# Retention's rotated queries and keys: 32x32 squares on VectorE and DMA moves in place of TensorE transposes

## The reference

```python
q = rotary(q.reshape(shp).astype(F32))                       # 256 tokens, 4 heads of 128
k = rotary(k.reshape(shp).astype(F32)) * (RET_HD ** -0.5)
...
scores = jnp.einsum("bhqd,bhkd->bhqk", qi, ki) * mask[None]
out = (jnp.einsum("bhqk,bhke->bhqe", scores, vi)
       + jnp.einsum("bhcd,bhde->bhce", qi * q_dec_f, state))
...
o = (o - mu) * lax.rsqrt(jnp.mean(jnp.square(o - mu), axis=-1, keepdims=True) + EPS)
```

## Time and profile before

| | us |
|---|---|
| median of 3 runs | 1694.01 (1693.87 to 1696.77) |
| span of the profiled execution | 1692.8 |
| TensorE busy | 1670.1 (99%) |
| VectorE busy | 1152.0 (68%) |
| ScalarE busy | 968.3 (57%) |
| span less TensorE busy | 22.7 |

### The profile page before, as it was taken

One profiled execution on the slowest core, in us unless ns is written; L12 is line 12 of the kernel. 1 busy time (PEld: TensorE's weight loads), 2 busy tenths in 40 slices (PEclk: granted clock), 3 DMA queues, 4 the chain that ended last, 5 costly groups with the idle time before them and its releaser, 6 DMA issues.

```text
span 1692.8 us, 24538 instructions
## 1 busy us (share of the span) xinstructions
PE 1670.1 (99%) x10066; PEld 1383.8 (82%) x10066; DVE 1152.0 (68%) x1835; ACT 968.3 (57%) x1522; POOL 19.9 (1%) x54
## 2 busy tenths in 40 slices
PE   9999999999999999999999999999999999999998
PEld 7778888887888888888888888888888888888886
DVE  6887875778788667555676578655575556985554
ACT  7845554577374447444667676544464456975443
POOL 1000000010000000000000000000000000000000
PEclk9999999999999999999999999999999999999999
DMA  7323355542244555455544335555555555455553
GB/s 265 125 82 132 147 183 187 178 169 107 77 168 162 180 196 188 178 195 177 210 185 153 134 124 177 218 194 190 208 192 194 181 217 187 149 187 180 193 180 143
DMA packets 41872, 291.67 MB, mean 172 GB/s; under 512 B 4673, under 2 KB 4929, under 8 KB 7713
## 3 DMA queue, kind: packets, MB, share of 16 engines
q1 hardware_dynamic: 39312, 280.68, 46.0%
q0 software_dynamic: 2304, 8.91, 1.5%
q10 hardware_dynamic: 144, 0.52, 0.1%
HBM read 289.05 MB, written 1.05 MB: 171 GB/s over the span
## 4 chain that ended last, share of the span: by engine, by line
PE 84%; DVE 10%; ACT 3%; issue 1%; DMA 1%; SPq 0%; DVEq 0%; ACTq 0%
PE pg L535 21%; PE pg L538 21%; PE pg L536 21%; PE pg L485 4%; PE pg L487 3%; PE pg L486 3%; DVE wl L2004 3%; PE ps L843 2%; PE ps L678 2%; DMA raw<-weights 1%; ACT wh L1339 1%; PE ps L892 1%; PE ps L662 1%; PE ps L964 0%; DVE hTl L2603 0%
## 5 line engine op out<-in xcount | busy, mean ns | idle before, releaser
L2004 DVE TENSOR_TENSOR wl<-raw,wh 128x1024 fp32r<-128x1024 f32 x494 | 581.3, 1220 | 183.7 <-ACT wh L1339 180.6
L535 PE MATMUL pg<-wh,hTh 128*128 128x512 f32 x1676 | 661.0, 394 | 1.3 <-ACT arena L1391 1.0
L538 PE MATMUL pg<-wh,hTl 128*128 128x512 f32 x1676 | 653.4, 390 | 0.0
L536 PE MATMUL pg<-wl,hTh 128*128 128x512 f32 x1676 | 652.5, 389 | 0.0
L1339 ACT ACTIVATE wh<-raw 128x1024 fp32r<-128x1024 f32 x522 | 522.8, 1054 | 201.7 <-DMA raw<-weights 191.4
L538 PEld LDWEIGHTS pg<-wh,hTl 128*128 128x128 f32 x1676 | 314.5, 188 | 67.0 <-DVE hTl L2070 0.3
L535 PEld LDWEIGHTS pg<-wh,hTh 128*128 128x128 f32 x1676 | 314.8, 188 | 64.0 <-ACT arena L1391 1.4
L536 PEld LDWEIGHTS pg<-wl,hTh 128*128 128x128 f32 x1676 | 315.0, 188 | 62.2
L485 PE MATMUL pg<-wh,hTh 128*128 128x512 f32 x416 | 171.4, 412 | 2.2 <-DVE wl L2004 2.2
L1445 ACT ACTIVATE arena<-pg,sm 128x256 f32<-128x256 f32 (+1 forms) x67 | 36.6, 547 | 237.4 <-PE pg L538 237.3
L487 PE MATMUL pg<-wh,hTl 128*128 128x512 f32 x416 | 163.0, 392 | 0.0
(11 more groups left out here) (406 smaller groups left out, 1322.7 us busy)
## 6 DMA issues: line engine op xcount, KB each, us to landing
raw<-weights SPq DMA_DIRECT2D x265, 1024.0 KB, 4.8
arena<-wide POOLq DMA_DIRECT2D x9, 512.0 KB, 3.7
raw<-weights SPq DMA_DIRECT2D x2, 512.0 KB, 6.4
cst<-const_tables POOLq DMA_DIRECT2D x1, 1024.0 KB, 5.3
plainh<-dist_tables POOLq DMA_DIRECT2D x2, 512.0 KB, 6.2
arena<-gate_mix POOLq DMA_DIRECT2D x1, 1024.0 KB, 8.3
x<-x_in ACTq DMA_DIRECT2D x1, 512.0 KB, 3.9
x<-x_in SPq DMA_DIRECT2D x1, 512.0 KB, 9.5
```

The lines of the kernel that those rows point to most:

```text
L535: pe.matmul(dst, high, wh[:, slot, at], start=start, stop=False)
L536: pe.matmul(dst, high, wl[:, slot, at], start=False, stop=False)
L538: return pe.matmul(dst, low, wh[:, slot, at], start=False, stop=stop)
L2004: tt(wl[:, slot, h], raw[:, slot, h], wh[:, slot, h], ALU.subtract)\
```

## The change

The 16 transposes of queries and keys on TensorE in each layer, and the four ScalarE copies out of PSUM, go. VectorE, right behind each `rotate`, transposes the result within 32x32 squares: two instructions of 128x512 for the queries, two for the keys. A 32x32 square that has been turned in place still lies in the wrong partitions, so SP moves squares between partitions by DMA from SBUF to SBUF: 16 DMAs of 32 partitions x 256 float32 (32 KB) for the queries, 16 for the keys, in four lots of eight that stand in SP's program behind weight units 21, 22, 23 and 24 of the layer. Their order leaves the tokens in an order of its own in the free dimension: for the queries the score product reads and writes with a rearranged pattern, and for the keys ScalarE makes one copy of 128x1024 that restores the order and applies the scale. That copy waits for all 32 moves (`rope_moved`) and stands between the sixth and the last two of the eight `AFTER_RESULT` steps in ScalarE's program. On TensorE the scores wait for `rope_moved` and for the copy.

```diff
@@ constants
+        ROPE_MOVES, LAYER_UNITS = 16, 22 + 12 + 6 + 4
+        ROPE_AT = (21, 22, 23, 24)
+        ROPE_SQUARES, ROPE_FEATS = (V(10240), V(6144)), (V(3072), V(1024))
+        def rope_features(t):
+            return ROPE_FEATS[t].rearrange("p (a h m t) -> p h m a t", a=4, h=NH, m=M)
@@ TensorE, retention
-                for t, src in enumerate((V(0), V(1024))):
-                    if t:
-                        prepare(BETWEEN_TURNS)
-                    c.wait("rope_done")
-                    v = src.rearrange("p (m d) -> p m d", m=M)
-                    for h in range(NH):
-                        for m in range(M):
-                            last = pe.transpose(ps[:, 2 * t + h // 2, ((h % 2) * M + m) * P:((h % 2) * M + m + 1) * P],
-                                                v[:, m, h * P:(h + 1) * P], ident)
-                    last.then_inc(sem["feat_tr"], 1)
-                prepare(BEFORE_RESULT)
-                c.wait("feat_read", 2)
+                prepare(BETWEEN_TURNS + BEFORE_RESULT)
...
-                kT, qT = V(2048).rearrange("p (h s) -> p h s", h=NH), V(3072).rearrange("p (h s) -> p h s", h=NH)
+                c.wait("rope_moved", 2 * 16 * ROPE_MOVES)
+                c.wait("feat_read")
+                qT, kT = rope_features(0), V(2048).rearrange("p (h s) -> p h s", h=NH)
...
-                        last = pe.matmul(ps[:, b, jm * S:(jm + 1) * S], kT[:, h, jm * P:(jm + 1) * P], qT[:, h, :],
-                                         start=True, stop=True)
+                        last = pe.matmul(ps[:, b, jm * S:(jm + 1) * S].rearrange("p (m a t) -> p m a t", m=M, a=4),
+                                         kT[:, h, jm * P:(jm + 1) * P], qT[:, h], start=True, stop=True)
@@ ScalarE, retention
-                for t, dst in enumerate((V(3072), V(2048))):
...
-                prepare(BEFORE_RESULT)
+                prepare(BETWEEN_TURNS + BEFORE_RESULT)
                 transpose_split(NH, 8, lambda k: fp("gdn_g"))
-                prepare(AFTER_RESULT)
+                prepare(AFTER_RESULT - 2)
+                c.wait("rope_moved", 2 * 16 * ROPE_MOVES)
+                act.activation(V(2048).rearrange("p (h m a t) -> p (h m) a t", h=NH, m=M, a=4),
+                               ROPE_FEATS[1].rearrange("p (a q t) -> p q a t", a=4, t=32), ACT.Copy, scale=HD ** -0.5)\
+                   .then_inc(sem["feat_read"], 1)
+                prepare(2)
@@ VectorE, delta_result
-                c.sig(rotate(RET_Q, V(0)), "rope_done")
-                pump(st.used + 4)
-                c.sig(rotate(RET_K, V(1024)), "rope_done")
+                for t, src in enumerate((RET_Q, RET_K)):
+                    if t:
+                        pump(st.used + 4)
+                    c.step(rotate(src, V(1024 * t)))
+                    to = ROPE_SQUARES[t].rearrange("p (j h m t) -> p m h j t", j=4, h=NH, m=M)
+                    for m in range(M):
+                        last = dve.transpose(to[:, m], V(1024 * t)[:, 512 * m:512 * m + 512]
+                                             .rearrange("p (h j t) -> p h j t", h=NH, j=4))
+                    last.then_inc(sem["rope_done"], 1)
@@ SP
+            rope_at = {LAYER_UNITS * l + u: (l, i // 2, i % 2) for l in range(DEPTH) for i, u in enumerate(ROPE_AT)}
+            def move_rope(l, t, i):
+                sp.wait_ge(sem["rope_done"], 2 * l + t + 1)
+                src, dst = ROPE_SQUARES[t], ROPE_FEATS[t]
+                for a in (2 * i, 2 * i + 1):
+                    for jj in range(4):
+                        sp.dma_start(dst[32 * jj:32 * jj + 32, S * a:S * a + S], src[32 * a:32 * a + 32, S * jj:S * jj + S])\
+                          .then_inc(sem["rope_moved"], 16)
...
                 if u:
                     sp.dma_start(raw[:, u % SPLIT_SLOTS, :], weights[u]).then_inc(weight_landed[u % SPLIT_SLOTS], 16)
+                if u in rope_at:
+                    move_rope(*rope_at[u])
```

More of the change, by code:

```diff
@@ L278, in program @@
             "o_sum", "norms_ready", "kn_ready", "zeros_ready", "inv_copied", "vs_ready", "mask_first", "probs_t", "probs_t_read", "product_sq", "qk_done", "qs_done", "r_ready", "rec_out",
-            "rope_done", "row_done", "rs_ready", "rv_ready", "sc_masked", "sc_ready", "small_done",
+            "rope_done", "rope_moved", "row_done", "rs_ready", "rv_ready", "sc_masked", "sc_ready", "small_done",
             "small_read", "small_copied", "small_turned", "small_w_high", "small_w_low", "split_high", "split_low", "sq_done", "sq_free",
@@ L1588, in retention @@
                 prepare(PREPARE_AFTER_SCAN)
-                for t, dst in enumerate((V(3072), V(2048))):
[L1590 to L1596, removed]
-                prepare(BEFORE_RESULT)
-                transpose_split(NH, 8, lambda k: fp("gdn_g"))
-                prepare(AFTER_RESULT)
+                prepare(BETWEEN_TURNS + BEFORE_RESULT)
+                transpose_split(NH, 8, lambda k: fp("gdn_g"))
+                prepare(AFTER_RESULT - 2)
[4 more added lines that the diff above has]
+                prepare(2)
             def merge_out():
```

## The result

The changed kernel takes **1714.2 us** (median of 4, 1712.77 to 1715.62) against 1694.2 for the kernel before beside it: a ratio of 1.0116 (95% interval 1.0102 to 1.0131), 20.0 us slower. The direction was forecast; the time lies 7.4 us above the 1706.8 predicted and 0.7 us above the end of its range. The profiled execution took 1713.28 us, its span is 1711.5; that is 18.7 more than the span in the earlier trace rows.

What follows compares the result with a forecast made beforehand. VectorE was taken to set the pace around retention, though TensorE is 99% busy. Transposes 2.4 plus later mask 3.9 made 6.4 us a layer, 12.8 in the run: 1694.0 + 12.8 = 1706.8 us, range 1701.5 to 1713.5.

Steps and rivals of the forecast that it cites:

- What sets the pace: Around retention, 158.04 to 184.02 us in the first layer: VectorE sets the pace for some 26 us per layer, not TensorE.
- TensorE's saved 3.5 us: Retention's transposes leaving TensorE: 3.5 us in the run, 1.76 a layer, become waiting before `y_ready`, worth 0.
- the sum: Both retention stages: 2.4 for VectorE's transposes plus 3.9 for the later first mask, 6.4 us a layer, 12.8 in all.
- the moves' issue pitch: SP's issues of the last eight moves behind unit 24: claimed to follow each other by 0.46 us.
- the clock: TensorE around retention: granted clock expected to stay at 1.00, so a fall adds nothing to the sum.
- VectorE's transposes: VectorE's pace-setting stretch before retention: four transposes of 128x512 at 0.61 us each, 2.4 us a layer (1.4 to 4.6).
- The moves: The keys' last eight moves behind unit 24: last one issued at 193.5 and landed at 195.9, in old times.
- The landing: Last move of the keys, behind unit 24: 2.4 us from issue to landing, so landed at 195.9.
- the upper end of 196.9: Upper end for the landing of the keys' last move, taken as 195.9, in old times.
- Copy, unit 23's split, mask: Behind the moves: copy done 196.9, ScalarE's split 198.9, VectorE's half and hand-overs 200.2; first mask 3.9 us later.
- the copy's upper end: ScalarE's copy of the keys, taken as 1.0 us: at most one more copy time, 1.0 us.
- the clock's rival: Idle TensorE before `y_ready` drops to 1.2 GHz: 2.7 us a layer, 5.5 in the run, 1712.3 us; chance 0.2.

Runs made afterwards that it cites:

- removed part alone: The kernel before without retention's 32 TensorE transposes and the ScalarE copies out of PSUM, nothing in their place: 1696.69 us, ratio 1.0014.
- The run with the split ahead: The kernel after with ScalarE splitting weight unit 23 ahead of the copy of the keys, not behind it: 1710.26 us, ratio 1.0094.
- the one with early moves: The kernel after with the keys' last eight moves issued behind weight unit 23, not behind unit 24: 1702.59 us, ratio 1.0047.
- both gaps filled: The kernel after with 15 unread TensorE products ahead of the result's transposes and 15 ahead of the scores: 1707.46 us, ratio 1.0076.
- the longer chain alone: The kernel before plus VectorE's four transposes of 128x512 a layer, whose output nobody reads: 1699.64 us, ratio 1.0032.
- with that one filled: The kernel after with 15 unread TensorE products ahead of the result's transposes only: 1711.12 us, ratio 1.0096.
- the sums on ScalarE: ScalarE sums the squares, VectorE's reduction goes: 1692.32 us on the kernel before, 1699.97 on the kernel after with early moves and one filler; text doesn't say which.
- GpSimd: The kernel before with the ten instructions of the keys' rotation moved from VectorE to GpSimd: 1704.31 us, ratio 1.0062.
- early moves and a filler: The kernel after with the keys' last eight moves behind unit 23 and 15 unread products ahead of the result's transposes: 1699.55 us, ratio 1.0033.

## Why the prediction was right and wrong

**What sets the pace: right.** VectorE's stretch did, and TensorE's saved 3.5 us were worth nothing (removed part alone: no gain). Two terms of the sum failed: the moves' issue pitch, and the clock, which it put at nothing.

**VectorE's transposes: right.** 0.62 us each for the 0.61 taken from a two-input operation of the same shape; all of the 2.4 us a layer reached the resumption. Alone they cost 5.4 us by the medians, 4.8 by the trace.

**The moves: mis-sized.** The step that failed here is the issue pitch. Instead of 0.46, from SP's first instructions of the run, it was 0.62: eight took 4.94 us. The last move started at 194.89 + 4.94 - 0.59 = 199.24, so 4.73 after unit 24's issue, not 3.55: **1.2 us a layer**. The landing held for the last move, 201.61 - 199.24 = 2.37 for the 2.4 taken; the median of all 64 is 3.1. In the old times the copy started at 189.91 + 7.10 = 197.0, just past the upper end of 196.9.

**Copy, unit 23's split, mask: right.** 4.31 us from the copy's start to the mask, for 4.3. The run with the split ahead gives 4 us back, and the one with early moves takes away both waits.

**The clock: the step that made the result miss its range.** The prediction saw the gap (3.6 us), named the fall and gave it 0.2, because "most work is dense" and no row showed a longer gap. It came in both layers of the profiled execution. That step failed: the fall was left out of the sum. Its price was worked out as 5.5 us; it is 3.9 by the traces and 6.7 by the medians. With both gaps filled the same program takes 1707.5, within 0.7 us of the forecast's 1706.8: the sum comes out for a clock that stays up, but in part by luck, since two misses nearly cancel. A layer came out 0.9 higher than the 6.4 of the sum (7.30, and 7.4 in the second), 14.7 for the run. Between the two stages 1.6 us of this are given back by the missing wait for "issue", so the spans differ by only 13.3.

**The range.** Its upper end, 1713.5, was set by the forecast's own bounds. The text names one more copy time, 1.0 us, as the copy's upper end, but the 9.5 us a layer leaves it out; with it the end is near 1715, above the measured time. And the clock's rival was said to lie inside at 1712.3. That rival was worked out on the central sum alone. A fall of 5.5 on top of moves at the measured pitch (+2.4) gives 1706.8 + 2.4 + 5.5 = 1714.7; measured was 1714.2. A rival that adds to the forecast has to be added to its bounds as well.

## What to carry to other kernels

Before taking work off the busiest engine, look whether it waits at the end of that stretch: here 32 transposes less were worth nothing. Together with VectorE's longer chain they left a gap of 3.56 us, and the clock fell behind it; the removal alone and the longer chain alone left gaps of 1.2 and 1.4 us and no fall there. When a chain gets a step on an in-order engine, write down what is queued behind the new wait, and behind which transfer its last input is issued; moving eight DMA issues forward by one unit gave back 11.6 of 20 us. An idle gap of some 3 us on TensorE is to be priced with its clock at 1.2 GHz behind it, as the likely case, and a filler in one gap doesn't price it while another one is open.

## What the hardware showed that I had not expected

The clock fell behind a gap of 3.56 us ahead of transposes, in both layers, and, with that one filled, behind gaps of 2.80 and 2.96 us ahead of the scores. Behind 2.89 us at the same place of the kernel after, where it had already fallen and risen once, it stayed at 1.00 in the profiled execution. Which gap is followed by a fall is thus not settled by its length alone in these runs.

It also fell where TensorE hardly waited (busy 3.87 of 4.00 us in the window below). In the delta net, some 100 us ahead of retention in each layer, TensorE does 96 small products in a row. In six of the twelve profiled executions the clock fell there: in both layers without the transposes, in the first with early moves, with the sums on ScalarE and with GpSimd, in the second with two fillers and with early moves and a filler. First the second half of these products in the kernel before and in the one without the transposes, then a window of the kernel with two fillers:

```profile
70.80 2.42 PE L820 MATMUL ps<-arena 128*64 128x64 f32 x64
70.58 3.20 PE L820 MATMUL ps<-arena 128*64 128x64 f32 x64
...
396.00:400.00 4.00, 3.87 (x59) 3.33 (x55) 3.92 (x6) 1.95 (x3) 0.00 (x0) 0.63 0.01 4
```

It cost nothing in those executions: VectorE is the busy engine there too (3.92 of 4.00 us), and the weight unit issued at 97.00 in the kernel before goes out at 96.77 in the one without the transposes. A mean clock below 1.00 is thus no price by itself.

SP's pitch for moves of 32 KB within SBUF, 0.62 us, is longer than for half units of 512 KB at the run's start (0.46), 16 times their size. A unit of 1 MB took 0.33 us to issue alone (194.51) and 0.58 between two lots of moves (182.01), as much as a move; so what stood ahead in the queue shows in the issue time, and the size doesn't. GpSimd and VectorE working at the same time on two-input operations brought VectorE's from a pitch of 0.34 to 0.88 us. And a kernel with less work and the same profiled span had a median 2.4 us higher; this stays open.
